# A query projection moved ahead of two seven-product projections, in a hybrid attention and mixture-of-experts layer

## The chip, the cores and the metric
The kernel runs on one core of one Trainium2 chip. The metric is the device time of one execution in microseconds (us); shown is the median of three runs. Profiles are taken from one more execution by the hardware profiler. TensorE (PE) does matrix products, VectorE (DVE), ScalarE (ACT) and GpSimd (POOL) work element by element, and SyncE (SP) issues most of the DMAs. Each engine works through its own queue in order, and they wait for each other through semaphores.

## The reference, cut to what matters
One layer over 256 latent tokens and 256 context tokens of width 1024, all in float32:

```python
zl, zc = split_in(h_lat @ w_in), split_in(h_ctx @ w_in)
na_q, na_k, na_v = zl[0:3]            # neighbourhood attention; keys and values of the context from zc
a_lat = neighbourhood_attention(na_q, na_k, na_v, na_kc, na_vc, rpb)
o_lat, _, _ = hgrn2_scans(zl[3], zl[4], zl[5], zl[6], lb, s_fwd, s_bwd)   # gated scan, values from zl[6]
...
y_lat = branch_merge((a_lat, b_lat, c_lat), zl[11:14], w_branch, w_out)
x = x + mod[2] * y_lat                # mod = silu(c) @ w_ada + b_ada, six column groups
...
x = x + mod[5] * hierarchical_moe(f_lat, ...)      # 16 experts
```

What the change touches are the projections of the neighbourhood queries (`nq`, latent tokens only), of the scan's values (`hi`), of the neighbourhood keys (`nk`) and values (`nv`), the last three over all 512 tokens, and the part of `mod` that GpSimd computes.

## The kernel before, in words
The order of the work is written out by hand for each engine. `FRONT` lists the weight blocks of the front part, 2 MB each, in the order in which SP loads them. They go round three places in memory (`SLOT_OF`), so a load waits until the block three places before it has been multiplied.

**TensorE.** Most projections are "fills": one bank of 512 columns each, eight matmuls for each 128 output columns. `hi`, `nk` and `nv` are computed instead with seven products of half-size blocks in place of eight (`SEVEN`; `first` to `seventh`, each issued by `part_product`, L944). Some products need sums of weight blocks (`sixth`, `seventh`, `fifth` and `third` do), which GpSimd makes. `third` needs the last of these. The fills of `nq` are issued by L908. Between these stand the `level(v)` steps of the gated scan (L1011), eight of them: DVE masks the result of a level (`products`, L1640) and scales its operands for a later one (`join`, L1652, L1653, L1656), ACT copies keys (`level_keys`, L756), and then comes the next level. So the projections fill the time in which TensorE would wait for DVE. `ctx_state` (L1043), `across` (L1022) and `outputs` end the scan. The attention steps, the branches, the output projection and the experts follow.

**GpSimd.** After sums of the tokens (L592 to L595) it works through 32 parts of the `mod` weights (512 KB each, two buffers, loaded by SP in order behind the weight blocks; `PARTS_BEHIND` says how many behind which block, and a part is issued when the one two before it is used). A part is multiplied by the conditioning vector, either with one `tensor_tensor` against a broadcast (L644) or with two `tensor_scalar` whose scalar is a pointer (L642), and then summed: one addition for the first part of a column group (L647), two for the other three (L649, L650). Between certain parts stand `weight_sums(name)` (three operations over 1024 elements, L606, L608, L609) and `last_weight_sum(name)` (one, L616), which change the weights of `hi`, `nk` and `nv` in place.

**DVE.** Behind the forget gates come the products for the context keys (L1593 to L1609), L1611 to L1617, four copies of turned context keys out of the shared banks (L1619), and then the levels. The seven products of `hi`, `nk` and `nv` are added up between the levels (`sums_of_first` and so on, L1680). TensorE's `first` and `fourth` wait until banks that they write have been read by these sums.

The waits of `third`, in full:

```python
pe.wait_ge(sums_ready, operand_no(name, 4))
pe.wait_ge(part_copied, SEVEN.index(name) + 1)
```

Of the kernel before, what the change touches and what calls it, by code (L numbers as in the profile page):

```python
# [39 lines left out]
ROUTES = GCOLS + NE  # L40


FRONT = ["ff", "fb", "hq", "hg", "hi", "nk", "nq", "nv", "gq", "gkv"]
FRONT += [f"gate{i}" for i in range(6)]
FRONT += ["br0", "br1", "br2", "out0", "out1"]
FSLOTS = 3
# [34 lines left out]
def sums_no(name, last):  # L81

    return 7 * SEVEN.index(name) + last
# [20 lines left out]
FILLS += [(f"out{i}", t, "dve") for t in range(NT) for i in range(2)]  # L104
PBANKS = 3
WARM = (7, 4, 1, 3)
BANK_OF = [{("ff", 3): 7, ("nq", 0): 0, ("nq", 1): 2}.get(f[:2], n % PBANKS) for n, f in enumerate(FILLS)]
ROW_GROUPS = (4, 5, 10, 11)
POOLED = (6, 7, 8, 9, 4, 5, 10, 11)
LOOP_SUMS = 6  # L110
PARTS = 4
PART_K = KD // PARTS
PARTS_BEHIND = {name: range(4 * i, 4 * i + 4) for i, name in enumerate(("hq", "hg", "hi", "nk", "nq", "nv"))}
PARTS_BEHIND["gq"], PARTS_BEHIND["gate0"] = range(24, 26), range(26, 32)


def fill_no(name, i=0):
    return [f[:2] for f in FILLS].index((name, i))
# [27 lines left out]
LEVELS = 8  # L146
# [22 lines left out]
def build(nc, d):  # L169

    ctx = ExitStack()
    with ctx:
# [113 lines left out]
        sums = keep(32)  # L286
# [104 lines left out]
        def wait_emptied(eng, n):  # L391

            who, count_ = emptied(n)
            eng.wait_ge(out_by[who], count_)
# [177 lines left out]
        def _(pool):  # L572
# [45 lines left out]

            pool.wait_ge(c_ready, 1)
            for q in range(PARTS * len(POOLED)):  # L620
                if q == 9:
                    weight_sums("hi")
                if q == 12:
                    last_weight_sum("hi")
                if q == 14:
                    weight_sums("nk")
                if q == 16:
                    last_weight_sum("nk")
                if q == 20:
                    weight_sums("nv")  # L630
                if q == 24:
                    last_weight_sum("nv")
                g, k0 = POOLED[q // PARTS], q % PARTS * PART_K
                pool.wait_ge(ada_in[q % 2], 16 * (q // 2 + 1))
                if q == LOOP_SUMS * PARTS:
                    pool.wait_ge(xy_ready, LEVELS + 2)
                if q == 4 * PARTS:
                    pool.wait_ge(shared_out, shared_no("kc", 3) + 1)
                w = ada_part[q % 2].rearrange("p (k c) -> p k c", k=PART_K)
                if 11 <= q < 20:  # L640
                    for k in range(PART_K):
                        last = pool.tensor_scalar(w[:, k, :], w[:, k, :], cvec[:, k0 + k, 0:1], None, ALU.mult)  # L642
                else:
                    last = pool.tensor_tensor(w, w, cvec[:, k0:k0 + PART_K, 0:1].broadcast_to([P, PART_K, 512]), ALU.mult)  # L644
                link(last)
                if k0 == 0:
                    ins = pool.tensor_tensor(ada_sum[g], w[:, 0, :], w[:, 1, :], ALU.add)  # L647
                else:
                    link(pool.tensor_tensor(w[:, 0, :], w[:, 0, :], w[:, 1, :], ALU.add))  # L649
                    ins = pool.tensor_tensor(ada_sum[g], ada_sum[g], w[:, 0, :], ALU.add)  # L650
                ins.then_inc(ada_part_used, 1)
                pool.wait_ge(ada_part_used, q + 1)
                if q % PARTS == PARTS - 1:
                    pool.sem_inc(ada_summed, 1)
# [48 lines left out]
        def _(act):  # L703
# [21 lines left out]
            def fill(n):  # L725

                name, i, who = FILLS[n]
                assert who == "act"
                ps = banks[BANK_OF[n]]
                act.wait_ge(fill_ready, n + 1)  # L730
                two = ps[:, :].rearrange("p (a b) -> p a b", a=2)
                done = out_by["act"]
                if name in ("ff", "fb"):
                    act.activation(forget[:, :, 4 * (name == "fb") + i, :], two, ACT.Sigmoid).then_inc(done, 1)
                elif name in ("hq", "hg"):
                    raw, sig = (QR, sig_q) if name == "hq" else (bT, sig_g)
                    act.activation(raw[:, 2 * i:2 * i + 2, :], two, ACT.Copy)
                    act.activation(sig[:, 2 * i:2 * i + 2, :], two, ACT.Sigmoid).then_inc(done, 1)
                elif name == "nq":
                    act.activation(na_q[:, 2 * i:2 * i + 2, :], two, ACT.Copy, scale=QSCALE).then_inc(done, 1)  # L740
                elif name == "gq":
                    act.activation(gq[:, i, :], ps[:, :], ACT.Copy).then_inc(done, 1)
                elif name == "gkv":
                    act.activation(gkv[:, 2 * i:2 * i + 2, :], two, ACT.Copy).then_inc(done, 1)
                elif name[:4] == "gate":
                    c = 4 * int(name[4:]) + 2 * i
                    if c == 0:
                        act.wait_ge(shared_out, shared_no("s0", 1) + 1)
                    act.activation(gates[:, c:c + 2, :], two, ACT.Copy).then_inc(done, 1)
# [13 lines left out]
                act.activation(out_part(name, 0, 0), product_bank(name, 1)[:, :].rearrange("p (a b) -> p a b", a=2),  # L763
                               ACT.Copy).then_inc(part_copied, 1)

            for n in range(fill_no("hi")):
                fill(n)
            level_keys(1)
            for v in range(LEVELS):
                if 0 < v < LEVELS - 1:  # L770
                    level_keys(v + 1)
                if v == 1:
                    copy_first("hi")
                if v == 4:
                    copy_first("nk")
            fill(fill_no("nq", 0))
            fill(fill_no("nq", 1))
            copy_first("nv")

            act.wait_ge(shared_out, shared_no("o", 1) + 1)  # L780
# [98 lines left out]
        def _(pe):  # L879
# [7 lines left out]
            def fill(n, ks=range(KD)):  # L887
# [3 lines left out]
                before = [m for m in range(n) if BANK_OF[m] == BANK_OF[n]]  # L891
                if before and ks[0] == 0:
                    wait_emptied(pe, before[-1])
                if name == "nq":
                    pe.wait_ge(out_by["sums"], sums_no("nk", 4))
                if name == "gq":
                    wait_emptied(pe, fill_no("nv"))
                g = FRONT.index(name)
# [48 lines left out]
            def first(name):  # L947

                take_slot(FRONT.index(name))
                if name == "hi":  # L950
                    wait_emptied(pe, fill_no("hg", 1))
                    pe.wait_ge(mix_out, MIXES)
                if name == "nk":
                    pe.wait_ge(out_by["sums"], sums_no("hi", 4))
                if name == "nv":
                    wait_emptied(pe, fill_no("nk"))
                part_product(name, 1, w_part(name, 0, 0), x_part(0, 0))

            def fourth(name):

                pe.wait_ge(sums_ready, 1)
                if name == "nk":
                    wait_emptied(pe, fill_no("hi"))
                if name == "nv":
                    wait_emptied(pe, fill_no("nq", 1))
                part_product(name, 4, w_part(name, 1, 1), x_sums[2])

            def second(name):
# [229 lines left out]
            fill(fill_no("hg", 1))  # L1198
            ctx_keys((2, 3))
            level(0)  # L1200
            first("hi")
            fourth("hi")
            level(1)
            second("hi")
            sixth("hi")
            level(2)
            seventh("hi")
            fifth("hi")
            level(3)
            third("hi")  # L1210
            first("nk")
            level(4)
            fourth("nk")
            second("nk")
            level(5)
            sixth("nk")
            seventh("nk")
            level(6)
            fifth("nk")
            third("nk")  # L1220
            level(7)
            fill(fill_no("nq", 0))
            ctx_state()
            fill(fill_no("nq", 1))
            across()
            first("nv")
            fourth("nv")
# [290 lines left out]
        def _(dve):  # L1518
# [169 lines left out]
            def sums_of_seventh(name):  # L1688

                add_product(name, 3, 7, 5, (1, 1), (0, 1))  # L1690
                add_product(name, 4, 4, 2, (1, 0), (1, 1))
# [12 lines left out]
            for v in range(1, LEVELS):  # L1704
                products(v)
                dve.wait_ge(v_step, steps[0])
                dve.wait_ge(xy_ready, v + 1)
                join(v)
                if v == 2:
                    sums_of_first("hi")  # L1710
                    sums_of_seventh("hi")
                if v == 3:
                    sums_of_fifth("hi")
                    sum_of_third("hi")
                if v == 5:
                    sums_of_first("nk")
                if v == 6:
                    sums_of_seventh("nk")
                    sums_of_fifth("nk")
                if v == LEVELS - 1:  # L1720
                    sum_of_third("nk")

            for q in range(2):
                shared_copy(shared_no("s0", q), S0[:, 4 * q:4 * q + 4, :].rearrange("p a b -> p (a b)"))
            for dr in range(2):
                shared_copy(shared_no("lev8", dr), AT[:, NT + dr, :])
            dve.wait_ge(v_step, steps[0])
# [557 lines left out]
```

## Time and profile before

| | |
|---|---|
| median of three runs | 698.49 us (697.67 to 698.77) |
| the profiled execution | 697.12 us |
| its span, first to last instruction | 695.1 us |
| TensorE busy | 679.4 us, 98% |
| VectorE busy | 325.3 us, 47% |
| GpSimd busy | 239.1 us, 34% |
| ScalarE busy | 106.7 us, 15% |
| mean granted clock of TensorE | 0.997 |

Busy times are sums over instructions; matmuls are pipelined and their ends are modelled, so TensorE's share says how closely its instructions follow each other. The trace counts two records for each float32 matmul. A busy share is an average: GpSimd is busy nearly all of the time from 47 to 232 us and little behind it. "Granted clock" is the share of full speed (2.4 GHz) that the chip grants TensorE.

### The profile page before, as it was taken

How to read it: one execution, taken by the hardware profiler on the slowest of the kernel's cores; microseconds unless marked ns; L12 is line 12 of the kernel's file. 1: busy time of each engine (PE TensorE's matmuls, PEld its weight loads, DVE VectorE, ACT ScalarE, POOL GpSimd, SP SyncE). 2: the span in 40 equal slices, each digit the busy share in tenths (PEclk: the TensorE clock that was granted, in tenths of full speed). 3: DMA queues.
4: the chain of work that ended last, by engine and by line, in shares of the span. 5: the costliest groups of instructions: out<-in, count | busy, mean ns of one | idle time of the engine just before them, and what ended most of it. 6: DMA issues, size and time to landing. Idle time of an engine off the chain costs nothing.

```text
span 695.1 us, 8395 instructions
## 1 busy us (share of the span) xinstructions
PE 679.4 (98%) x3432; PEld 445.6 (64%) x3432; DVE 325.3 (47%) x531; ACT 106.7 (15%) x188; POOL 239.1 (34%) x155
## 2 busy tenths in 40 slices
PE   9999999999999999999999999999999999999995
PEld 5444587979989567777877888667435534434431
DVE  3459697796632687754343233336303203202214
ACT  4011011111001222321221140013000000000013
POOL 0029999999999594800000000000000000000014
PEclk9999999999999999999999999999999999999998
DMA  8993551341417744433491149866999999999993
GB/s 353 416 407 101 211 227 74 140 180 61 185 59 270 305 128 172 186 122 121 180 410 60 78 134 424 350 256 237 397 417 423 418 422 421 420 421 421 421 414 132
DMA packets 29512, 183.74 MB, mean 264 GB/s; under 512 B 3543, under 2 KB 5975, under 8 KB 14624
## 3 DMA queue, kind: packets, MB, share of 16 engines
q1 hardware_dynamic: 27456, 178.72, 64.7%
q0 software_dynamic: 1584, 3.97, 1.5%
q8 instruction: 29, 0.48, 0.3%
q10 hardware_dynamic: 432, 0.49, 0.2%
q14 instruction: 11, 0.09, 0.0%
HBM read 178.15 MB, written 6.82 MB: 266 GB/s over the span
## 4 chain that ended last, share of the span: by engine, by line
PE 75%; POOL 15%; DMA 4%; DVE 3%; issue 2%; ACT 1%; SPq 0%; POOLq 0%; DVEq 0%
PE bank L1431 21%; PE bank L908 14%; PE bank L944 6%; PE bank L925 6%; PE bank L1389 4%; POOL sb L644 3%; PE bank L931 3%; PE bank L1190 3%; PE bank L1113 2%; POOL sb L650 2%; PE bank L1136 2%; POOL sb L649 2%; PE bank L912 2%; PE bank L1121 2%; POOL sb L642 2%
## 5 line engine op out<-in xcount | busy, mean ns | idle before, releaser
L1431 PE MATMUL bank<-sb 128*64 128x512 f32 x768 | 166.8, 594 | 0.7 <-ACT sb L837 0.7
L685 POOL DMA_INDIRECT y_rows<-sb,token_rows x7 | 7.0, 1002 | 359.9 <-DVE sb L2049 335.1
L908 PE MATMUL bank<-sb 128*128 128x256 f32 x576 | 128.1, 381 | 0.0
L1431 PEld LDWEIGHTS bank<-sb 128*64 128x64 f32 x768 | 54.3, 137 | 106.5 <-issue 103.7
L908 PEld LDWEIGHTS bank<-sb 128*128 128x128 f32 x576 | 108.4, 190 | 16.2 <-issue 2.4
L944 PE MATMUL bank<-sb 128*128 128x256 f32 x336 | 74.1, 380 | 1.6 <-POOL sb L609 1.6
L944 PEld LDWEIGHTS bank<-sb 128*128 128x128 f32 x336 | 63.3, 190 | 9.9 <-POOL sb L609 1.8
L1619 DVE COPY sb<-bank 128x512 f32<-128x512 f32 x45 | 29.2, 684 | 82.5 <-PE bank L1121 54.4
L2009 DVE TENSOR_TENSOR sb<-sb,bank 128x512 f32<-128x512 f32 x8 | 5.5, 688 | 99.0 <-PE bank L1431 99.0
L644 POOL TENSOR_TENSOR sb<-sb 128x1024 f32<-128x1024 f32 x23 | 47.8, 2076 | 9.5 <-DMA sb<-ada_w 7.7
L925 PE MATMUL bank<-sb 128*128 128x256 f32 x192 | 41.9, 380 | 0.0
L925 PEld LDWEIGHTS bank<-sb 128*128 128x128 f32 x192 | 36.4, 190 | 5.0 <-issue 0.2
L650 POOL TENSOR_TENSOR sb<-sb 128x512 f32<-128x512 f32 x24 | 34.8, 1449 | 1.9
L642 POOL TENSOR_SCALAR sb<-sb 128x512 f32<-128x512 f32 x18 | 34.8, 1944 | 0.6
L649 POOL TENSOR_TENSOR sb<-sb 128x512 f32<-128x512 f32 x24 | 32.0, 1332 | 1.9
L2000 DVE TENSOR_SCALAR sb<-bank,sb 128x128 f32<-128x128 f32 x64 | 21.8, 404 | 17.8 <-PE bank L1389 17.6
L1190 PE MATMUL bank<-sb 128*128 128x512 f32 x64 | 29.0, 599 | 0.7 <-DVE sb L1571 0.7
L1389 PE MATMUL bank<-sb 128*128 128x128 f32 x224 | 27.9, 278 | 0.0
L904 PE MATMUL bank<-sb 128*128 128x512 f32 x64 | 27.6, 592 | 0.0
L792 ACT ACTIVATE sb<-bank,sb 128x512 f32<-128x512 f32 x32 | 21.8, 685 | 37.1 <-DVE sb L1784 37.1
L1389 PEld LDWEIGHTS bank<-sb 128*128 128x128 f32 x224 | 26.1, 192 | 0.0
L2049 DVE SCALAR_TENSOR_TENSOR sb<-bank,sb 128x512 f32<-128x512 f32 x14 | 10.5, 751 | 26.9 <-PE bank L1431 26.9
(260 smaller groups left out, 810.8 us busy)
## 6 DMA issues: line engine op xcount, KB each, us to landing
sb<-expert_w SPq DMA_DIRECT2D x90, 1024.0 KB, 17.6
sb<-front_w SPq DMA_DIRECT2D x19, 2048.0 KB, 8.4
sb<-ada_w SPq DMA_DIRECT2D x32, 512.0 KB, 3.7
sb<-ada_mix SPq DMA_DIRECT2D x4, 2048.0 KB, 19.8
sb<-expert_w SPq DMA_DIRECT2D x12, 512.0 KB, 10.9
sb<-xcT SPq DMA_DIRECT2D x4, 512.0 KB, 6.4
sb<-front_w SPq DMA_DIRECT2D x4, 512.0 KB, 20.5
y_rows<-sb SPq DMA_DIRECT2D x4, 512.0 KB, 24.0
```

What stands on the lines that cost most here:

```text
L642: last = pool.tensor_scalar(w[:, k, :], w[:, k, :], cvec[:, k0 + k, 0:1], None, ALU.mult)
L644: last = pool.tensor_tensor(w, w, cvec[:, k0:k0 + PART_K, 0:1].broadcast_to([P, PART_K, 512]), ALU.mult)
L649: link(pool.tensor_tensor(w[:, 0, :], w[:, 0, :], w[:, 1, :], ALU.add))
L650: ins = pool.tensor_tensor(ada_sum[g], ada_sum[g], w[:, 0, :], ALU.add)
L904: ins = pe.matmul(ps[:, :], lhs(w, k, i * P), hT[:, k, :], start=(k == 0), stop=(k == KD - 1))
L908: ins = pe.matmul(ps[:, c * L:(c + 1) * L], lhs(w, k, (2 * i + c) * P), hT[:, k, 0:L], start=(k == 0), stop=(k == KD - 1))
L925: ins = pe.matmul(ps[:, c * L:(c + 1) * L], lhs(w, k, (2 * i + c) * P, D), src[:, k, :], start=(k == 0), stop=(k == 3))
L944: ins = pe.matmul(o, left, right, start=(k == 0), stop=(k == 3))
L1190: ins = pe.matmul(banks[BANK_OF[i]][:, :], lhs(slot[0], k, i * P), hT[:, k, :], start=(k == 0), stop=(k == KD - 1))
L1389: ins = pe.matmul(banks[i][:, c * P:(c + 1) * P], x_nat[:, t, (4 * i + c) * P:(4 * i + c + 1) * P], S[:, t, :], start=(t == 0), stop=(t == ...
L1431: ins = pe.matmul(bank[e * CAP:(e + 1) * CAP, :], lhsT[:, k, e * CAP:(e + 1) * CAP], weights_at(k, e), start=(k == 0), stop=(k == parts - 1))
L1619: dve.tensor_copy(dst, shared_wait(n)[:, :]).then_inc(shared_out, 1)
```

## The change
The fills of `nq` move from behind level 7 to behind level 0 and level 1. The products of `hi` and `nk` come two levels later; the last four of `nk` stand behind level 7, two on each side of `ctx_state`, the last right ahead of `across`. `nq` is loaded ahead of `hi` and `nk`. ACT's and DVE's steps that go with them move alike; two waits of TensorE that belonged to the old places go, two others come. On GpSimd the sums of weights move behind later parts: `hi` from 9 and 12 to 13 and 16, `nk` from 14 and 16 to 18 and 21, `nv` from 20 and 24 to 24 and 26. The pointer form of the multiply, used for the parts 11 to 19, is used for 5 to 19.

```diff
-FRONT = ["ff", "fb", "hq", "hg", "hi", "nk", "nq", "nv", "gq", "gkv"]
+FRONT = ["ff", "fb", "hq", "hg", "nq", "hi", "nk", "nv", "gq", "gkv"]
...
-BANK_OF = [{("ff", 3): 7, ("nq", 0): 0, ("nq", 1): 2}.get(f[:2], n % PBANKS) for n, f in enumerate(FILLS)]
+BANK_OF = [7 if f[:2] == ("ff", 3) else n % PBANKS for n, f in enumerate(FILLS)]
...
-PARTS_BEHIND = {name: range(4 * i, 4 * i + 4) for i, name in enumerate(("hq", "hg", "hi", "nk", "nq", "nv"))}
+PARTS_BEHIND = {name: range(4 * i, 4 * i + 4) for i, name in enumerate(("hq", "hg", "nq", "hi", "nk", "nv"))}
...
             for q in range(PARTS * len(POOLED)):
-                if q == 9:
+                if q == 13:
                     weight_sums("hi")
-                if q == 12:
+                if q == 16:
                     last_weight_sum("hi")
-                if q == 14:
+                if q == 18:
                     weight_sums("nk")
-                if q == 16:
+                if q == 21:
                     last_weight_sum("nk")
-                if q == 20:
+                if q == 24:
                     weight_sums("nv")
-                if q == 24:
+                if q == 26:
                     last_weight_sum("nv")
...
-                if 11 <= q < 20:
+                if 5 <= q < 20:
...
                 if 0 < v < LEVELS - 1:
                     level_keys(v + 1)
-                if v == 1:
+                if v < 2:
+                    fill(fill_no("nq", v))
+                if v == 3:
                     copy_first("hi")
-                if v == 4:
+                if v == 6:
                     copy_first("nk")
-            fill(fill_no("nq", 0))
-            fill(fill_no("nq", 1))
...
-                if name == "nq":
-                    pe.wait_ge(out_by["sums"], sums_no("nk", 4))
...
                 if name == "hi":
-                    wait_emptied(pe, fill_no("hg", 1))
+                    wait_emptied(pe, fill_no("nq", 0))
...
+                if name == "hi":
+                    wait_emptied(pe, fill_no("nq", 1))
...
-                if name == "nv":
-                    wait_emptied(pe, fill_no("nq", 1))
...
             level(0)
+            fill(fill_no("nq", 0))
+            level(1)
+            fill(fill_no("nq", 1))
+            level(2)
             first("hi")
             fourth("hi")
-            level(1)
+            level(3)
             second("hi")
             sixth("hi")
-            level(2)
+            level(4)
             seventh("hi")
             fifth("hi")
-            level(3)
+            level(5)
             third("hi")
             first("nk")
-            level(4)
+            level(6)
             fourth("nk")
             second("nk")
-            level(5)
+            level(7)
             sixth("nk")
             seventh("nk")
-            level(6)
+            ctx_state()
             fifth("nk")
             third("nk")
-            level(7)
-            fill(fill_no("nq", 0))
-            ctx_state()
-            fill(fill_no("nq", 1))
             across()
...
-                if v == 2:
+                if v == 4:
                     sums_of_first("hi")
                     sums_of_seventh("hi")
-                if v == 3:
+                if v == 5:
                     sums_of_fifth("hi")
                     sum_of_third("hi")
-                if v == 5:
-                    sums_of_first("nk")
-                if v == 6:
-                    sums_of_seventh("nk")
-                    sums_of_fifth("nk")
-                if v == LEVELS - 1:
-                    sum_of_third("nk")
+            sums_of_first("nk")
+            sums_of_seventh("nk")
 
             for q in range(2):
                 shared_copy(shared_no("s0", q), S0[:, 4 * q:4 * q + 4, :].rearrange("p a b -> p (a b)"))
+            sums_of_fifth("nk")
+            sum_of_third("nk")
```

## Rows read from the trace of the kernel before

**Rows 1.** The page, busy us of each engine, share of the span, instructions.

```profile
PE 679.4 (98%) x3432; PEld 445.6 (64%) x3432; DVE 325.3 (47%) x531; ACT 106.7 (15%) x188; POOL 239.1 (34%) x155
```

**Rows 2.** The chain that ended last: start us, us, what.

```profile
151.43 2.51 POOL sb L609
...
161.20 1.78 PE bank L1011 x16
...
180.37 6.91 PE bank L908 x32
187.28 3.57 PE bank L1043 x32
...
217.05 13.81 PE bank L944 x64
```

**Rows 3.** TensorE's timeline: start us, us, instruction, records, idle time before and releaser.

```profile
1.33 5.16 PE L1164 MATMUL bank<-sb 128*128 128x256 f32 x14 [1.33 <-DVE sb L1532]
...
13.24 1.89 PE L1164 MATMUL bank<-sb 128*128 128x256 f32 x8
...
112.81 1.17 PE L1032 MATMUL bank<-sb 128*128 128x128 f32 x8 [1.26 <-DVE sb L1619]
...
154.05 7.15 PE L944 MATMUL bank<-sb 128*128 128x256 f32 x32 [1.62 <-POOL sb L609]
...
171.51 7.07 PE L944 MATMUL bank<-sb 128*128 128x256 f32 x32
...
197.60 1.95 PE L1022 MATMUL bank<-sb 128*128 128x128 f32 x16
```

**Rows 4.** VectorE's timeline, 108 to 157 us.

```profile
108.70 3.37 DVE L1617 TENSOR_TENSOR sb<-sb 128x1024 f32<-128x1024 f32 x1
...
151.64 2.27 DVE L1680 TENSOR_TENSOR sb<-bank,sb 128x512 f32<-128x512 f32 x3
...
155.05 1.21 DVE L1652 TENSOR_TENSOR sb<-sb 128x1024 f32<-128x1024 f32 x1
```

**Rows 5.** GpSimd's timeline, starts of parts and sums, 80 to 228 us.

```profile
80.18 1.89 POOL L644 TENSOR_TENSOR sb<-sb 128x1024 f32<-128x1024 f32 x1
...
122.15 3.12 POOL L642 TENSOR_SCALAR sb<-sb 128x512 f32<-128x512 f32 x2
...
170.59 3.10 POOL L642 TENSOR_SCALAR sb<-sb 128x512 f32<-128x512 f32 x2
...
175.14 3.98 POOL L642 TENSOR_SCALAR sb<-sb 128x512 f32<-128x512 f32 x2
...
181.92 5.00 POOL L642 TENSOR_SCALAR sb<-sb 128x512 f32<-128x512 f32 x2
...
189.72 3.10 POOL L642 TENSOR_SCALAR sb<-sb 128x512 f32<-128x512 f32 x2
...
194.24 1.27 POOL L650 TENSOR_TENSOR sb<-sb 128x512 f32<-128x512 f32 x1
195.75 2.35 POOL L606 TENSOR_TENSOR sb<-sb 128x1024 f32<-128x1024 f32 x1 [0.24 <-POOL sb L650]
...
208.09 1.90 POOL L644 TENSOR_TENSOR sb<-sb 128x1024 f32<-128x1024 f32 x1
...
212.75 1.90 POOL L644 TENSOR_TENSOR sb<-sb 128x1024 f32<-128x1024 f32 x1
...
224.56 1.89 POOL L644 TENSOR_TENSOR sb<-sb 128x1024 f32<-128x1024 f32 x1
...
227.88 1.90 POOL L644 TENSOR_TENSOR sb<-sb 128x1024 f32<-128x1024 f32 x1
```

**Rows 6.** Windows: us, busy us of PE, PEld, DVE, ACT, POOL, granted clock, DMA.

```profile
687.00:688.00 1.00, 0.61 (x2) 0.00 (x0) 0.83 (x2) 0.97 (x4) 1.00 (x2) 1.00 0.00 0
...
691.00:692.00 1.00, 0.00 (x0) 0.00 (x0) 0.00 (x0) 0.00 (x0) 0.00 (x0) 0.61 0.52 184
```

**Rows 7.** DMA issues, 100 to 240 us: count, KB each, median us to landing.

```profile
sb<-front_w SPq DMA_DIRECT2D x5, 2048.0 KB, 8.2
```

More of the change, by code:

```diff
@@ L764, in copy_first @@
                                ACT.Copy).then_inc(part_copied, 1)
-            for n in range(fill_no("hi")):
+            for n in range(fill_no("nq")):
                 fill(n)
```

## The prediction, as put on record
> **What bounds the kernel now.** I read the page first. TensorE is busy for 98% of the span [rows 1], so the question is where it waits, and whether the new order makes it wait more. In the chain that ended last, followed in order of time, the reader is to see that from the operand sums at 47 us to 154 us the chain runs over GpSimd, and that behind L609 it crosses to TensorE and stays there up to the attention stage [rows 2]. GpSimd is thus the second engine that can set the end. TensorE's timeline shows two idle times between 110 and 232 us: 1.26 us at 112.81 and 1.62 us at 154.05 [rows 3]. Everything else of this stretch is back to back: a product of the seven takes 13.81/4 = 3.45 us, a half of a query projection 3.45 us per 128 columns (6.91 a fill), a level 1.78 us, the context state 3.57 us [rows 2].
>
> The 1.26 us is TensorE's ctx_keys((2, 3)) behind DVE's copy L1619, which stands behind four two-input operations that GpSimd's weight sums had stretched: L1617 took 3.37 us, while the same kind of operation with the same number of elements took 1.21 us beside a tensor_scalar of GpSimd [rows 4]. The 1.62 us is put down to GpSimd L609, but fourth("nk") doesn't wait for it. It waits for the sums of "hi" on DVE, whose last three (L1680, from 151.64, 2.27 us) ended at 153.91, the same moment [rows 3, 4].
>
> **What the change moves.** Between the start of level(0) and the start of across() TensorE issues the same instructions before and after: eight levels, four query halves in two fills, twelve of the products with their two thirds, and the context state. Only their order differs. If nothing waited, across() would start at 197.60 - 1.26 - 1.62 = 194.72 [rows 3], and third("nk"), which now stands right in front of it, at 194.72 - 3.45 = 191.27. third("hi") stands before it by itself, first("nk"), level 6, two products, level 7, two products, the context state and fifth("nk"): 3.45 + 3.45 + 1.78 + 6.91 + 1.78 + 6.91 + 3.57 + 3.45 = 31.30 us, so it would start at 159.97. These are the two due times for GpSimd: third(name) needs last_weight_sum(name).
>
> In the kernel before, last_weight_sum("nk") was done when part 16 began, at 170.59 [rows 5], and third("nk") started at 171.51 + 3.45 = 174.96 [rows 3]: 4.4 us to spare. The change puts third("nk") later on TensorE by 191.27 - 174.96 = 16.3 us. It puts the last sum of "nk" behind five more parts (16 to 20). In the trace of before, these took from 170.59 to 195.75 (parts 16 to 19), and part 20, a first one in the tensor_tensor form, 3.32 us more: 28.5 us. By this alone the sum comes 28.5 - 4.4 - 16.3 = 7.8 us too late. This difference of the two displacements is the core of the forecast; the change of form adds to it.
>
> **GpSimd's work, term by term** [rows 5]. Undisturbed, a part that isn't the first of its column group costs 5.90 us with pointer multiplies (189.72 to 194.24 + 1.27 = 195.51, and 0.11 to the next), and 4.66 with one tensor_tensor (208.09 to 212.75). The first of a group costs 4.55 (170.59 to 175.14) and 3.32 (224.56 to 227.88). An operand sum costs 2.35 (195.75), so weight_sums with its gaps 7.2 and the last sum 2.35. So each of the six parts 5 to 10 that change form costs 1.24 us more, 7.4 in all, if nothing disturbs.
> From the start of part 5 (80.18), up to which nothing changes, to the end of last_weight_sum("nk") GpSimd now has twelve later parts and three first ones with pointers, part 20, two weight_sums, two last sums and four waits of 0.24: 12 x 5.90 + 3 x 4.55 + 3.32 + 14.4 + 4.7 + 1.0 = 107.9. Undisturbed it ends at 188.05.
> It isn't undisturbed. Before, 80.18 to 122.15 held five later parts and one first one of the old form and a weight_sums: 5 x 4.66 + 3.32 + 7.2 + 0.24 = 34.1 of 41.97 us, so 7.9 us went to sharing with DVE. 122.15 to 195.75 held 7 x 5.90 + 2 x 4.55 + 7.2 + 4.7 and 1.3 of waits = 63.6 of 73.6 us: 10.0 us. DVE's joins and sums of that second stretch all fall before the last sum of "nk" in the new order too, so I keep the 10.0. Of the 7.9 I keep 4.5, between nothing and the whole: DVE's four operations L1611 to L1617 run up to 2.1 us faster each beside pointer multiplies [rows 4], so DVE is through by about 105 instead of 112, and parts 9 to 11 run nearly alone. The sum is 188.05 + 10.0 + 4.5 = 202.5; the ends are 188.05 (no sharing) and 206.0 (all of it).
>
> A rule beside this: the Trainium skill, "SBUF — State Buffer", Who interferes with whom, says that a DVE instruction with two SBUF inputs and a reading GpSimd instruction exclude each other, and that the second blocks for the whole of the first. The seven joins of the second stretch issue fourteen such instructions of 1.21 us; by that rule GpSimd could lose all their 17 us in place of 10.0, and the time would be some 7 us above my forecast. The trace bears out that both engines slow down, and shows less than the whole on GpSimd.
>
> **What TensorE then does.** third("hi") waits first. GpSimd reaches the end of its last sum at 80.18 + 9 x 5.90 + 2 x 4.55 + 7.2 + 2.35 + 0.5 = 152.4, plus 4.5, plus some 6 of the 10.0: near 163, so 2 to 3 us idle. Behind it in TensorE's queue stand all later levels, but DVE's next join isn't what sets the end any more. third("nk") waits until 202.5 against 191.3 + 3: an idle time near 8 us. These waits don't add: what sets across() is 202.5 + 0.1 + 3.45 = 206.05, which is 8.45 us later than 197.60. Any stall in front of it (a join of level 2 stretched by weight_sums("hi"), for one) is swallowed by it, and so are the 2.9 us that the two old idle times give back.
>
> Then the clock. Behind TensorE's last matmul (busy for 0.61 us of the slice from 687) the granted clock was 0.61 of full in the slice 691 to 692 [rows 6], so it fell from 2.4 to 1.2 GHz after 3 to 4 us of idleness. An idle time near 8 us should do the same. What the return costs no row shows directly. Bounds: 0, and the nearest row, the first 14 matmul records of the kernel, 5.16 us where eight of the same form later took 1.89 [rows 3]: 5.16 - 14 x 0.22 = 2.0 us lost. I take 2.0, as a start from rest is nearest. The Trainium skill, "TensorE: Matmul & The Clock Gate", Part 1, says that idleness throttles the array to 1.2 GHz and that sustained activity releases it; the first half agrees with the row.
>
> The third value projection doesn't add. Behind the last sum of "nk" GpSimd has three later parts of the old form, weight_sums("nv"), parts 24 and 25 and the last sum: 14.0 + 7.4 + 3.3 + 4.7 + 2.6 = 32.0, and about 1.2 for the last join: 235.7. TensorE comes to third("nv") 217.05 + 10.36 - 197.76 = 29.65 us behind the start of across() [rows 2, 3], at 206.05 + 29.65 + 2.0 = 237.7. Without the clock's 2.0 it would be a tie; this is the next wait in line.
> At nothing I cost: the removed waits of "nq" and "nv" (others of the same banks were long done), the moved ACT copies (idle for 7 to 10 us between levels), and the weights. SP issues each 2 MB load behind a part's use, 8.2 us to landing [rows 7]: "hi" would land near 122 and is due at 133, "nk" lands near 156 and is due at 163 or later, "nv" near 184 against 209. If parts ran 8 us later still, "nk" would be the next. Behind the seven products TensorE is busy up to the experts without a gap that could give the time back, and the expert stage is bound by TensorE too: the shift goes to the end in full.
>
> **Sum.** 8.45 + 2.0 = 10.5 us on the profiled execution: 697.12 + 10.5 = 707.6 (its span 695.1 and 2.0 around it). That execution lies 1.4 us under the median of the runs, 698.49, so for the median: 709.0.
>
> **The rivals.**
> A, a milder stall: GpSimd shares less with DVE and the last sum of "nk" ends at 195 to 200, the idle time is split over third("hi") and third("nk") in pieces too short for the clock. 197 gives 197 + 3.55 - 197.6 = +3: 701.5. For it: part 16 to 19 pointer pairs were sometimes not stretched at all (3.10 at 170.59). Against: 10 us were lost in the second stretch.
> B, the other side: GpSimd keeps its due time. The point is 194.05 for no change; from 191.2 down the two old idle times are all that counts, -2.9: 695.6. It needs nearly no sharing (188.05). That DVE is freed speaks for it; the difference of displacements, 7.8 us before any change of form, against.
> C, worse: pointer multiplies give way each time DVE wants the port. If all six new pairs stretch as the worst of before (181.92, 5.00 against 3.10 [rows 5]), 11.4 in place of 4.5: the sum ends at 209.5, and the time is 17.4 more with the clock's part, 716.
> If only the new form did nothing, the last sum would end at 191.3 + 7.8 = 199.1 and the shift be 5.0 in place of 8.45: a case of A.
>
> **Chances.** The forecast (+6.5 to +14) 0.60, A 0.20, B 0.09, C 0.11. The range goes to 701 and 716: it leaves out B, a fifth of A and half of C, 0.19. Runs of this kernel differ by 0.2% (1.4 us), so under that a change can't be told from none. Faster by more than that: 0.07 (most of B); within it: 0.03; slower: 0.90.
>
> **What the new profile would show.** TensorE idle before L944 near 195 to 203, released by GpSimd L616, longest wait 6 to 9 us, and a smaller one near 160 by the same line; no idle time at 112; L616 for "nk" ending near 202.5; L1611 to L1617 on DVE at 1.2 to 2.3 us; a granted clock under 1 in the slices around 203. It is wrong if L616 of "nk" ends before 194, if the longest wait names DVE or a DMA, or if the clock stays at 1 behind an idle time of 6 us and more.

## The result and the profile after

The changed kernel takes 709.46 us in the median of four runs (708.55 to 711.79), the kernel before 698.56 (698.49 in the median of three, one run more here). The medians differ by 10.9 us. The ratio that is used from here on is 1.0164, its 95% interval 1.0137 to 1.0190, which stands for 11.4 us slower. The profiled execution took 708.55 us with a span of 706.5, 11.4 above that of before.

The page of the changed kernel, busy times and the granted clock in 40 slices. TensorE's share falls from 98% to 97% [rows 1], GpSimd does 6.1 us more, DVE 6.9 us less, and the clock has one slice below 9, the tenth, besides the last one (an 8, in the kernel before too).

```profile
PE 682.2 (97%) x3432; PEld 447.2 (63%) x3432; DVE 318.4 (45%) x531; ACT 106.9 (15%) x188; POOL 245.2 (35%) x161
...
PEclk9999999997999999999999999999999999999998
```

Who TensorE waited for between 100 and 245 us (us in total, times, the longest). Line numbers above 890 are two lower than before, and L1619 is L1617.

```profile
PE bank L942 <- POOL sb L616: 11.2, 2, 7.8
PE bank L1009 <- DVE sb L1617: 0.4, 1, 0.4
```

The two idle times of before [rows 3] are gone, and two waits for last_weight_sum (L616) stand in their place. TensorE's timeline shows where:

```profile
111.52 1.04 PE L1030 MATMUL bank<-sb 128*128 128x128 f32 x8
...
167.29 9.90 PE L942 MATMUL bank<-sb 128*128 128x256 f32 x32 [7.80 <-POOL sb L616]
...
187.50 7.07 PE L942 MATMUL bank<-sb 128*128 128x256 f32 x32
...
205.04 3.72 PE L942 MATMUL bank<-sb 128*128 128x256 f32 x16 [3.44 <-POOL sb L616]
208.59 1.95 PE L1020 MATMUL bank<-sb 128*128 128x128 f32 x16
```

The row at 167.29 is third("hi") and first("nk"), that at 205.04 third("nk"), that at 208.59 across(). across() started at 197.60 before [rows 3]: 10.99 us of the 11.4 are there, in front of it. The row at 167.29 takes 9.90 us for 32 records where the one at 187.50 takes 7.07: the clock. Windows of the same execution, the granted clock behind the five busy times:

```profile
157.00:160.00 3.00, 2.49 (x20) 2.22 (x18) 1.90 (x4) 0.00 (x0) 2.90 (x3) 1.00 0.81 280
160.00:163.00 3.00, 0.00 (x0) 0.00 (x0) 3.00 (x3) 0.00 (x0) 2.84 (x3) 0.93 0.29 113
163.00:166.00 3.00, 0.00 (x0) 0.00 (x0) 2.90 (x4) 1.06 (x1) 2.76 (x2) 0.50 0.07 16
...
170.00:172.00 2.00, 2.00 (x6) 1.61 (x5) 0.00 (x0) 0.00 (x0) 1.82 (x3) 0.50 0.00 0
172.00:180.00 8.00, 8.00 (x44) 7.17 (x44) 2.42 (x4) 0.00 (x0) 7.76 (x5) 0.95 0.41 142
...
203.00:205.00 2.00, 0.00 (x0) 0.00 (x0) 0.13 (x1) 0.00 (x0) 2.00 (x2) 1.00 0.72 256
```

Within the idle time of 7.8 us the clock went to 1.2 GHz and stayed there for about the first 5.5 us of the work behind it, which cost 9.90 - 7.07 = 2.8 us. In the idle time of 3.4 us in front of 205 it stayed at 2.4 GHz.

GpSimd's timeline of the changed kernel, beginning with part 5. Compare its parts with [rows 5].

```profile
80.32 3.12 POOL L642 TENSOR_SCALAR sb<-sb 128x512 f32<-128x512 f32 x2
...
92.90 5.11 POOL L642 TENSOR_SCALAR sb<-sb 128x512 f32<-128x512 f32 x2
...
120.80 3.11 POOL L642 TENSOR_SCALAR sb<-sb 128x512 f32<-128x512 f32 x2
...
164.89 2.34 POOL L616 TENSOR_TENSOR sb<-sb 128x1024 f32<-128x1024 f32 x1 [0.24 <-POOL sb L650]
...
202.64 2.34 POOL L616 TENSOR_TENSOR sb<-sb 128x1024 f32<-128x1024 f32 x1
...
235.88 2.36 POOL L616 TENSOR_TENSOR sb<-sb 128x1024 f32<-128x1024 f32 x1
```

The last sum of "nk" ends at 202.64 + 2.34 = 204.98, and third("nk") starts 0.06 us later. That of "nv" ends at 238.24, which is when third("nv") was due on TensorE (227.89 + 10.36 = 238.25): the third due time is met without a margin.

### The profile page after: what moved, and what is told of

It reads as the page before. It is cut to its first block, busy times and chain, and to the rows that moved or that the text cites. A ratio compares the mean times of both kernels' runs of the same rounds, so it can differ in the third digit from the quotient of the medians.

```text
span 706.5 us, 8398 instructions
## 1 busy us (share of the span) xinstructions
PE 682.2 (97%) x3432; PEld 447.2 (63%) x3432; DVE 318.4 (45%) x531; ACT 106.9 (15%) x188; POOL 245.2 (35%) x161
## 4 chain that ended last, share of the span: by engine, by line
PE 69%; POOL 22%; DVE 3%; DMA 3%; issue 2%; ACT 1%; POOLq 0%; DVEq 0%
PE bank L1429 21%; PE bank L906 12%; POOL sb L642 8%; PE bank L923 6%; PE bank L942 4%; PE bank L1387 4%; POOL sb L650 3%; PE bank L929 3%; POOL sb L649 3%; PE bank L1188 3%; PE bank L1134 2%; PE bank L1111 2%; PE bank L910 2%; PE bank L1119 2%; POOL sb L644 2%
## 5 line engine op out<-in xcount | busy, mean ns | idle before, releaser
L906 PE MATMUL bank<-sb 128*128 128x256 f32 x576 | 128.1, 381 | 0.0
L942 PE MATMUL bank<-sb 128*128 128x256 f32 x336 | 77.2, 390 | 11.2 <-POOL sb L616 11.2
L1617 DVE COPY sb<-bank 128x512 f32<-128x512 f32 x45 | 29.1, 682 | 78.7 <-PE bank L1119 53.3
L642 POOL TENSOR_SCALAR sb<-sb 128x512 f32<-128x512 f32 x30 | 56.6, 1899 | 1.4 <-POOL sb L650 0.4
L923 PE MATMUL bank<-sb 128*128 128x256 f32 x192 | 41.9, 380 | 0.0
L644 POOL TENSOR_TENSOR sb<-sb 128x1024 f32<-128x1024 f32 x17 | 33.1, 1949 | 16.2 <-DMA sb<-ada_w 14.9
L650 POOL TENSOR_TENSOR sb<-sb 128x512 f32<-128x512 f32 x24 | 36.4, 1518 | 1.9
L649 POOL TENSOR_TENSOR sb<-sb 128x512 f32<-128x512 f32 x24 | 32.9, 1370 | 1.9
L1678 DVE TENSOR_TENSOR sb<-bank,sb 128x512 f32<-128x512 f32 x21 | 14.5, 690 | 26.0 <-PE bank L942 24.9
## 6 DMA issues: line engine op xcount, KB each, us to landing
sb<-expert_w SPq DMA_DIRECT2D x12, 512.0 KB, 10.9
```

Source lines behind the costliest of these rows:

```text
L906: ins = pe.matmul(ps[:, c * L:(c + 1) * L], lhs(w, k, (2 * i + c) * P), hT[:, k, 0:L], start=(k == 0), stop=(k == KD - 1))
L923: ins = pe.matmul(ps[:, c * L:(c + 1) * L], lhs(w, k, (2 * i + c) * P, D), src[:, k, :], start=(k == 0), stop=(k == 3))
L942: ins = pe.matmul(o, left, right, start=(k == 0), stop=(k == 3))
L1617: dve.tensor_copy(dst, shared_wait(n)[:, :]).then_inc(shared_out, 1)
```

## The experiments

Names: G is the theory that GpSimd's queue sets the time through the ends of the last sums; F, S and O are rivals, each told in the text in which it stands. Every ratio is to the kernel before on the same chip, whose median was 697.2 to 697.9 us there, about 1 us under that of the result.

**a1: the new places with the old form.**

```diff
-                if 5 <= q < 20:
+                if 11 <= q < 20:
```

> The changed kernel with the pointer form only for the parts 11 to 19, as before. Theory G (the place of the last sums on GpSimd sets the time): parts 5 to 10 took 40.5 us in the changed kernel and 32.2 in the kernel before (without its weight_sums), so the last sum of nk ends 8.3 us earlier, at 196.7, and across starts at 200.2, 2.6 us later than before; no wait at third(hi). TensorE idles some 5 us at third(nk); if the clock falls there, up to 2.8 us more. 701 to 704 us. Rival F (the pointer form is the cause): the time goes back to that of before or under it, 696 to 698.5.

706.27 us, ratio 1.0129 (1.0114 to 1.0145). The rival falls: without the new form the kernel is still 9 us slower. G gave too little (701 to 704 us, with across() at 200.2; it started at 206.95). TensorE's timeline and the last sum of "nk":

```profile
161.03 7.17 PE L942 MATMUL bank<-sb 128*128 128x256 f32 x32 [0.84 <-POOL sb L616]
...
201.91 5.21 PE L942 MATMUL bank<-sb 128*128 128x256 f32 x16 [7.58 <-POOL sb L616]
```

```profile
114.83 3.97 POOL L642 TENSOR_SCALAR sb<-sb 128x512 f32<-128x512 f32 x2
...
199.51 2.34 POOL L616 TENSOR_TENSOR sb<-sb 128x1024 f32<-128x1024 f32 x1
```

GpSimd began part 11 6.0 us earlier than in the changed kernel (114.83 against 120.80), but had only 3.1 us of that left at the last sum of "nk" (201.85 against 204.98): between the two its pairs of pointer multiplies were stretched more. In the changed kernel DVE worked through most of TensorE's wait of 7.8 us, but behind it had only 0.69 us of work up to the next level:

```profile
173.77 0.69 DVE L1678 TENSOR_TENSOR sb<-bank,sb 128x512 f32<-128x512 f32 x1 [7.64 <-PE bank L942]
178.12 0.74 DVE L1638 COPY_PREDICATED sb<-masks,bank 128x512 f32<-128x512 int8 x1 [3.65 <-PE bank L1009]
```

There the pair of part 16 took 3.11 us, against 5.13 in a1, where a join ran beside it. That this is where a1 lost its start is read from the timelines, and no run tests it alone. The idle time moved to third("nk"), the clock fell there, and its 1.5 us (5.21 against 3.72) count in full.

**a2: the sums of "hi" earlier, the others as changed.**

```diff
-                if q == 13:
+                if q == 12:
                     weight_sums("hi")
-                if q == 16:
+                if q == 14:
                     last_weight_sum("hi")
```

> The changed kernel with the sums of hi behind the parts 11 and 13 instead of 12 and 15. Theory G: the wait of 7.8 us at third(hi) and the clock loss of 2.8 us behind it go, but the work of GpSimd up to the last sum of nk is the same, so that ends at 205 again; TensorE now idles from about 191.5 to 205 at third(nk), the clock falls there, and its loss is no longer swallowed: 709.5 + 2.8 = 712 us. Rival S (waits and clock loss add up): 7.8 + 2.8 less, 699 us.

711.91 us, ratio 1.0207 (1.0191 to 1.0223). The wait at third("hi") is gone, and the kernel is 0.0043 of the time, 3.0 us, slower than the changed one. Its two waits on TensorE:

```profile
186.87 9.66 PE L942 MATMUL bank<-sb 128*128 128x256 f32 x32 [10.19 <-POOL sb L608]
...
206.68 6.54 PE L942 MATMUL bank<-sb 128*128 128x256 f32 x16 [3.12 <-POOL sb L616]
```

The idle time went to sixth("nk") (which waits for L608, the second operand sum) and third("nk"), where G had put all of it at third("nk"). The last sum of "nk" ended at 206.6, 1.6 us later than in the changed kernel and not at the same 205, and the last product ran at the low clock (6.54 us, against 3.72). So the time that G gave, 712, came, but not from the clock alone. Removing the longest wait made the kernel slower, as G said and adding up the waits did not.

**a4 and a7: TensorE kept busy.** a4 lets TensorE run 16 matmuls into a bank that has been read, ahead of third("hi"); a7 also 12 ahead of third("nk"). Their results are overwritten unused.

```diff
             level(5)
+            pe.wait_ge(out_by["sums"], sums_no("hi", 2))
+            for _ in range(16):
+                pe.matmul(part_bank[2][:, 0:256], ident, x_part(0, 0)[:, 0, :], start=True, stop=True)
             third("hi")
```

> The changed kernel with 16 more matmuls (6.9 us, their result is overwritten unused) ahead of third(hi), in the time in which TensorE waits for GpSimd. Theory G: the clock stays at full speed there, the 2.8 us behind it are not lost, but the last sum of nk still ends at 205: the same time, 709.5 us, or up to 2.8 more if the clock now falls in the longer idle time at third(nk) (6 us). Rival S (the clock loss is a part of the 11 us): 706.7 us.

> a4 with 12 more unused matmuls (5.2 us) ahead of third(nk) too. In a4 the clock fell at third(nk), and that product took 6.16 us instead of 3.62. Theory: full speed at both waits, across() starts 2.5 us earlier than in a4, 709.3 us, the same as the changed kernel within 1 us: its clock loss at third(hi) cost nothing. Rival: the clock loss at third(hi) is part of the changed kernel's time, then 706.7 us.

a4: 711.83 us, ratio 1.0208 (1.0193 to 1.0224). a7: 710.46 us, ratio 1.0177 (1.0159 to 1.0196). With a4 the work behind third("hi") ran at full speed, and TensorE then idled 6.98 us at third("nk"), where the clock fell:

```profile
167.95 7.17 PE L942 MATMUL bank<-sb 128*128 128x256 f32 x32 [0.89 <-POOL sb L616]
...
206.73 6.16 PE L942 MATMUL bank<-sb 128*128 128x256 f32 x16 [6.98 <-POOL sb L616]
```

a7 has no fall of the clock (mean 0.998, against 0.989 of the changed kernel):

```profile
206.66 3.72 PE L942 MATMUL bank<-sb 128*128 128x256 f32 x16 [1.82 <-POOL sb L616]
```

Its interval contains the ratio of the changed kernel and lies above what the rival's 706.7 us would give. So the 2.8 us at the low clock in the changed kernel cost nothing: TensorE had to wait again behind them. a4 shows the price if such a loss comes behind the last wait: across() started at 212.72 there and at 210.22 in a7, the 2.5 us that were expected. In both, the last sum of "nk" ended 1.6 to 1.7 us later than in the changed kernel, which goes with a7 lying 1.2 us above the 709.3 that were expected. Some 0.6 us of that were there before part 5; behind it the pair of part 18 took 5.13 us in place of 3.10:

```profile
187.02 5.13 POOL L642 TENSOR_SCALAR sb<-sb 128x512 f32<-128x512 f32 x2
```

**a5: the sums of "nk" earlier (17 and 18).**

```diff
-                if q == 18:
+                if q == 17:
                     weight_sums("nk")
-                if q == 21:
+                if q == 18:
                     last_weight_sum("nk")
```

> The changed kernel with the sums of nk alone earlier (17 and 18 instead of 18 and 21). Theory G: the wait of 3.4 us at third(nk) goes, but the work of GpSimd up to the last sum of nv is the same, and that ended at 238.24 in the changed kernel, the moment at which third(nv) was due; so nv now waits the 3.4 us: the same time as the changed kernel, 709.5 us (12 us over the kernel before of the same chip). Rival S (each wait removed is time gained): 3.4 less, 706 us.

709.40 us, ratio 1.0169 (1.0154 to 1.0184): the same as the changed kernel, as G said. third("nk") no longer waits, and the products of "nv" do. Of the 8.1 us below, 7.8 are still the wait of third("hi") and 0.3 that of third("nv"); the 4.0 us are a wait of sixth("nv") for its operand sum, where G had put the wait at third("nv"):

```profile
PE bank L942 <- POOL sb L616: 8.1, 2, 7.8
PE bank L942 <- POOL sb L608: 4.0, 1, 4.0
```

**b1: the kernel before with the new form alone.**

```diff
-                if 11 <= q < 20:
+                if 5 <= q < 20:
```

> The kernel before with one part of the change alone: the pointer form from part 5 on. Theory G: GpSimd comes some 6 us later to its last sums (between the changed kernel and a1, the start of part 11 moved by 6.0 us), which had 4.4 us to spare for nk and 2.6 for nv; so 3 to 4 us slower than the kernel before. Rival (the form is harmless, since DVE is freed and the 1.26 us at 112 go): the same or up to 1.3 us faster.

705.21 us, ratio 1.0114 (1.0099 to 1.0129): 7.9 us slower, where I expected 3 to 4.

```profile
177.53 2.34 POOL L616 TENSOR_TENSOR sb<-sb 128x1024 f32<-128x1024 f32 x1 [0.24 <-POOL sb L650]
```

```profile
179.92 6.61 PE L944 MATMUL bank<-sb 128*128 128x256 f32 x16 [7.72 <-POOL sb L616]
...
205.54 1.95 PE L1022 MATMUL bank<-sb 128*128 128x128 f32 x16
```

The last sum of "nk" ended at 179.87, 9.3 us later than before (170.59, [rows 5]), not 6. That is more than the 7.4 us which six parts cost undisturbed. 9.3 less the 4.4 to spare is 4.9, and 2.9 at the low clock (6.61 against 3.72) make 7.8; across() is 7.94 us later. That DVE was freed earned nothing at the due time. The form alone costs 7.9 us and the places alone (a1) 9.0, both together 11.4: the costs don't add. At across() the three are 7.94, 9.35 and 10.99 us, so 6.3 are missing. 4.4 of them are the clock: its falls cost 2.9 us in b1 and 1.5 in a1, each behind the last wait, and nothing in the changed kernel. Most of the rest is that the form puts third("nk") 5.0 us later in the old order (9.3 less the margin) and moves the last sum by 3.1 in the new one (201.85 to 204.98).

**a3: all sums earlier, new form** (hi 12 and 14, nk 17 and 18, nv 22 and 23).

> The changed kernel with all sums earlier: hi 12 and 14, nk 17 and 18, nv 22 and 23. Theory G: the last sums end near 152, 188 and 221 us against the due times 160, 191.3 and 224.3, so no wait and no fall of the clock is left, and the two idle times of before are gone too: 698.5 - 2.9 = 695.6 us. Rival O (the order of the products or of the DVE steps costs by itself): 700 us or more, with TensorE waiting for DVE or for itself.

707.63 us, ratio 1.0140 (1.0121 to 1.0159). G's number missed by 12 us; the rival's "700 or more" holds as a number, but not for its reason. Two things showed. sixth("nk") still waited, and the clock fell. And DVE waited 7.4 us for the attention bias, which no sum has to do with:

```profile
181.27 9.80 PE L942 MATMUL bank<-sb 128*128 128x256 f32 x32 [4.32 <-POOL sb L608]
...
201.39 1.95 PE L1020 MATMUL bank<-sb 128*128 128x128 f32 x16
```

```profile
242.75 0.43 DVE L1776 TENSOR_TENSOR bank<-bank,sb 128x256 f32<-128x256 f32 x1 [7.36 <-DMA sb<-na_bias]
```

The SP queue explains it. Part 25 is issued when part 23 has been used, and behind it in SP's order stand the gkv weights and the bias. In this kernel:

```profile
225.84 7.31 SPq L522 DMA_DIRECT2D sb<-ada_w  x2
233.19 0.43 SPq L510 DMA_DIRECT2D sb<-front_w  x1
233.66 0.43 SPq L518 DMA_DIRECT2D sb<-na_bias  x1
```

across() was 3.8 us later than before, the end 10.6: the other 6.8 us came behind it, and the wait for the bias is what changed there (a8 and a9 test it). Part 23 is a due time of GpSimd too, and pulling sums ahead of it spends that margin.

**a6: a3 with the old form.**

```diff
-                if 5 <= q < 20:
+                if 11 <= q < 20:
```

> a3 with the pointer form only from part 11 on. In a3 a third due time of GpSimd showed: SP issues the gkv weights and the attention bias behind part 25, and that behind part 23, whose end was 232.8; the bias landed at 242.7 and DVE waited 7.4 us. Theory G with this due time: the old form brings GpSimd 3 to 6 us forward, the bias lands at 237 to 239, no wait at the sums is left, and the time is 1 us under to 4 us over the kernel before. Rival O (the order of TensorE's work costs by itself): still 8 us or more over it.

700.96 us, ratio 1.0046 (1.0028 to 1.0064). No wait for a sum is left, and the new order of TensorE does what the unimpeded sum says:

```profile
195.40 1.95 PE L1020 MATMUL bank<-sb 128*128 128x128 f32 x16
```

195.40 against 197.60, 2.2 us earlier. Rival O falls: the order of the products and of DVE's steps together can cost no more than the 0.7 us that are missing to 194.72. DVE's wait for the bias is still 6.7 us, and gives the gain back and more. It makes TensorE wait three times in the attention stage (3.5 us together), and behind the last of these the clock is down:

```profile
239.87 0.66 PE L1119 MATMUL bank<-sb 128*128 128x128 f32 x4 [0.97 <-DVE sb L1786]
240.96 0.63 PE L1119 MATMUL bank<-sb 128*128 128x128 f32 x4 [0.43 <-DVE sb L1549]
244.76 0.82 PE L1101 MATMUL bank<-sb 128*128 128x128 f32 x4 [2.11 <-DVE sb L1617]
```

From 245 to 248 us the granted clock was 0.50 to 0.52, so the price of the bias includes a fall of the clock. In a3 it was 0.50 from 249 to 254. The seven executions fit this: 698.8 and 699.1 us at a mean clock of 0.998, 700.9 to 702.9 at 0.992 to 0.995.

**a8 and a9: the bias out of part 25's way**, in a6 and in a3.

```diff
-PARTS_BEHIND["gq"], PARTS_BEHIND["gate0"] = range(24, 26), range(26, 32)
+PARTS_BEHIND["gq"], PARTS_BEHIND["gkv"], PARTS_BEHIND["gate0"] = range(24, 25), range(25, 26), range(26, 32)
```

> a6 with part 25 of the mod weights issued by SP behind the attention bias instead of ahead of it, so that gkv and the bias don't stand behind part 23 of GpSimd. In a6 TensorE reached across() at 195.4, 2.2 us earlier than the kernel before, with no wait for a sum, and lost it to the bias (DVE waited 6.7 us). Theory: the bias is issued when fifth(nv) is done, near 225, lands near 231.5, and the 2.2 us stay: 2 us faster than the kernel before. Rival: another wait of the attention stage takes their place, and the time stays at 3 us over it.

> a3 (pointer form from part 5) with the same edit of SP's order. Theory: of a3's 10.6 us over the kernel before, 3.8 came ahead of the last value products (GpSimd's sums of nk) and 6.8 behind, from the bias; the 6.8 go: about 4 us over the kernel before. Rival: as for a8, 8 us or more.

a8: 696.09 us, ratio 0.9984 (0.9968 to 0.9999), 1.1 us faster than the kernel before: faster, but by less than the 0.2% that I hold to be safe. a9: 703.97 us, ratio 1.0075 (1.0052 to 1.0099), 5.2 us slower, against 9.8 in a3. SP's queue and TensorE in a8:

```profile
225.84 0.33 SPq L518 DMA_DIRECT2D sb<-na_bias  x1
227.16 0.33 SPq L522 DMA_DIRECT2D sb<-ada_w  x1
```

```profile
PE bank L1101 <- DVE sb L1617: 1.3, 2, 0.7
PE bank L1009 <- issue: 0.6, 1, 0.6
PE bank L1009 <- DVE sb L1617: 0.4, 1, 0.4
```

The bias is issued as soon as fifth("nv") is through, 7.8 us earlier than in a3, and both kernels give back most of what it had cost (0.0062 and 0.0065 of the time, 4.3 and 4.5 us). The profiled executions show it too. From across() to the attention product that starts at 265.18 us in the kernel before (L1101; at 276.08 in a3, 271.48 in a9), a3 loses 7.1 us and a9 1.4. Another 1.7 us of a9 are lost behind 683 us, and stay unexplained. a8 is the new order of TensorE with the placing and the form that GpSimd can keep.

## Why the prediction was right, point by point

**The core holds.** That the last sum of "nk" moves further on GpSimd (28.5 us) than third("nk") moves on TensorE (16.3) was the first reason, and the runs bear it out: a1 has the new places without the form, its last sum of "nk" ended 31.2 us later than before (201.85 against 170.61), and it is 9 us slower; a6 undoes the places and the form, and the waits are gone. The places suffice by themselves, but so does the form (b1, 7.9 us), which the prediction had as an addition. The unimpeded start of across() was put at 194.72, and a6 reached 195.40. The two idle times of before went, as said; DVE's L1611 to L1617 took 1.48, 2.30, 2.17 and 1.21 us, in the range that was given.

**Two terms were wrong, and cancelled.** The shift of across() was put at 8.45 + 2.0 for the clock, and was 10.99.
- The step that kept 4.5 of the 7.9 us of sharing was too small. The last sum of "nk" ended 124.7 us behind the start of part 5 (204.98 - 80.32), with 107.9 of work: 16.8 us of sharing, not 14.5. Up to the start of part 11 (120.80) it was 6.2 in place of 4.5, behind it 10.6 in place of 10.0. "Parts 9 to 11 run nearly alone" holds for 9 (3.11) and 11 (3.11), but the pair of part 7 took 5.11 us (the row at 92.90), beside DVE's L1609 and its neighbours.
- The step that put the clock's 2.0 us behind third("nk") failed at its place. I had a wait of 2 to 3 us at third("hi") and near 8 at third("nk"). They were 7.8 and 3.4. GpSimd reached the end of the last sum of "hi" at 167.2, not 163: by then 14.7 of the 16.8 us of sharing had been spent, where I had 10.5 of 14.5. The clock fell at the first wait and cost 2.8 us there, and a7 shows that these were swallowed by the second. So the clock's share in the result is zero, and the sum on GpSimd's side is 2.5 us larger. That the median came out within half a microsecond of 709.0 is luck of the size of these two; of the signs that I named, the clock under 1 near 203 didn't come (it was 1.00 there and 0.50 near 165), and the longest wait stood at third("hi").

**"These waits don't add"** was right, and is the best tested sentence: a2 takes away the longest wait and is slower by 3 us, a5 takes away the second and changes nothing.

**The next in line.** third("nv") was named as such, with 2 us to spare or a tie. It was a tie (238.24 against 238.25), and in a5 the products of "nv" waited. What the prediction missed is the due time of part 23: it costed SP's loads of "hi", "nk" and "nv", but not gkv and the bias behind part 25. In the changed kernel this cost nothing, since part 23 was used by 220.6 and the bias was issued at 238.44, when fifth("nv"), for which it also waits, was through. In a3 and a6 it was most of the loss behind across().

**The rivals.** A (a milder stall) fell with the last sum at 204.98. B asked for nearly no sharing, and b1 shows the form costing 9.3 us of GpSimd's time rather than less than its 7.4. C didn't come: the pairs of parts 5 to 10 took 3.1 to 5.1 us, not all 5.0. Nor did GpSimd lose all 17 us of DVE's fourteen two-input instructions: behind part 11 it lost 10.6.

**Open.** Why the form costs GpSimd 9.3 us in the old order and 3.1 in the new one isn't settled; it was only read from the timelines that it depends on which of DVE's instructions meet which part. a8 is 1.1 us faster where the unimpeded sum gives 2.9. In its profiled execution part 5 began 0.9 us later than before (81.11 against 80.18), TensorE idled 0.6 us in front of level 7 (the row "issue"), and 0.5 went in the attention stage; I didn't try to find their causes.

## What to carry to other kernels

When work is moved on one engine and its helper's work on another, compare the two displacements against the margin of before: what is left is the first term of the forecast. What an instruction of the helper costs in its new neighbourhood is the second, and here it was the less certain. A helper that runs one long queue has several due times, its sums and the loads that its progress lets out: relieving one spends the margin of the next, and only shortening the queue, or taking a load out from behind it, gives time back. A wait in front of a later wait for the same queue was free here, its low clock included (a7), and removing it cost time (a2).

## What the runs showed of the hardware that I had not expected

- The granted clock fell in idle times of TensorE from 10.19 us (a2) down to 3.12 us (a2 again), and in a6 behind one of 2.11 us, with two shorter ones (0.97 and 0.43) ahead of it. It stayed at full speed in one of 3.44 us (the changed kernel). So the length of the idle time alone doesn't say whether it falls.
- Nor does it say what a fall costs. Idle times of 7.6 to 7.8 us at one of the last sums cost the work behind them 1.5 us in a1 and a5 (7.07 to 8.59 for the same 32 records), 2.8 in the changed kernel and 2.9 in b1. Over all these runs a fall between 160 and 240 us cost 1.5 to 3.1 us (3.1 in a9, 10.18 against 7.07, behind 4.32 us of idleness). The 2.0 us worked out from the kernel's first matmuls lie in this range.
- A pair of pointer multiplies on GpSimd takes 3.10 us alone and up to 5.13 beside DVE. DVE's two-input instruction of 1024 elements mostly keeps its 1.21 us beside it (1.60 at most in the changed kernel), and takes up to 3.37 beside GpSimd's `tensor_tensor`. The form protects DVE at GpSimd's expense, and here it was GpSimd that was late.
